# Second mixer's attention: a minimum over negated scores as the exponential's bias, and fillers ahead of each transposition

## The reference

```
# neighbourhood attention, head h
s = q @ k.T * D ** -0.5 + bias[h]            # masked entries: -1e30
p = softmax(s);  o = p @ v
# sliding window attention, head h
s = where(band, q @ k.T * D ** -0.5, -1e30)
m = max(max(s), sink[h])
p = exp(s - m);  denom = sum(p) + exp(sink[h] - m)
o = (p / denom) @ v
# mixer
m = (sigmoid(gate_na) * (o_na @ w_na) + sigmoid(gate_sw) * (o_sw @ w_sw)) @ w_out
```

## Time and profile before

| | us |
|---|---|
| median of three runs | 2382.12 (2380.49 to 2384.36) |
| profiled execution | 2384.57 |
| its span | 2382.70 |
| TensorE busy | 2257.1 (95%) |
| VectorE busy | 1750.5 (73%) |
| ScalarE busy | 1476.7 (62%) |
| GpSimd busy | 236.8 (10%) |

### The profile page before, as it was taken

One profiled execution on the slowest core, in us unless ns is written; L12 is line 12 of the kernel. 1 busy time (PEld: TensorE's weight loads), 2 busy tenths in 40 slices (PEclk: granted clock), 3 DMA queues, 4 the chain that ended last, 5 costly groups with the idle time before them and its releaser, 6 DMA issues.

```text
span 2382.7 us, 31050 instructions
## 1 busy us (share of the span) xinstructions
PE 2257.1 (95%) x11606; PEld 1904.2 (80%) x11606; DVE 1750.5 (73%) x2374; ACT 1476.7 (62%) x2129; POOL 236.8 (10%) x142
## 2 busy tenths in 40 slices
PE   8889999878999999899999889999999999999997
PEld 7677888777788788788789778888888888888885
DVE  6755556773555566655566679999999999999998
ACT  5544445554544455444446568787878887788886
POOL 1431000232000242100215000000000000000000
PEclk9989999999999999999999989999999999999999
DMA  7314555512555534555554379999999999999996
GB/s 283 119 45 156 187 187 175 188 54 81 184 187 187 193 130 151 168 189 187 170 184 142 120 247 359 350 368 347 366 351 369 360 362 356 360 372 366 369 368 245
DMA packets 157276, 570.89 MB, mean 240 GB/s; under 512 B 18561, under 2 KB 18913, under 8 KB 156481
## 3 DMA queue, kind: packets, MB, share of 16 engines
q1 hardware_dynamic: 154032, 555.58, 65.8%
q0 software_dynamic: 3088, 13.27, 1.7%
HBM read 567.72 MB, written 1.05 MB: 239 GB/s over the span
## 4 chain that ended last, share of the span: by engine, by line
PE 84%; DVE 10%; ACT 3%; issue 2%; POOL 0%; DMA 0%; DVEq 0%; SPq 0%; POOLq 0%; ACTq 0%
PE bank L499 23%; PE bank L500 23%; PE bank L501 23%; PE bank L2005 2%; PE bank L2007 2%; PE bank L2006 2%; DVE w_lo L441 2%; PE bank L1631 2%; ACT w_hi L435 1%; PE bank L861 1%; PE bank L1000 1%; PE bank L2562 1%; PE bank L985 1%; DVE X L1889 1%; DVE small L678 1%
## 5 line engine op out<-in xcount | busy, mean ns | idle before, releaser
L441 DVE TENSOR_TENSOR w_lo<-raw,w_hi 128x1024 fp32r<-128x1024 f32 x986 | 1191.3, 1227 | 302.2 <-ACT w_hi L435 272.6
L435 ACT CAST w_hi<-raw 128x1024 fp32r<-128x1024 f32 x1055 | 1100.4, 1051 | 326.0 <-PE bank L501 272.0
L499 PE MATMUL bank<-w_hi,x_hi 128*128 128x512 f32 (+2 forms) x2144 | 843.2, 393 | 27.5 <-DVE w_lo L441 11.4
L500 PE MATMUL bank<-w_lo,x_hi 128*128 128x512 f32 (+2 forms) x2144 | 829.9, 387 | 0.0
L501 PE MATMUL bank<-w_hi,x_lo 128*128 128x512 f32 (+2 forms) x2144 | 829.1, 387 | 0.0
L499 PEld LDWEIGHTS bank<-w_hi,x_hi 128*128 128x128 f32 x2144 | 409.5, 191 | 107.8 <-DVE w_lo L441 9.6
L501 PEld LDWEIGHTS bank<-w_hi,x_lo 128*128 128x128 f32 x2144 | 408.6, 191 | 80.0
L500 PEld LDWEIGHTS bank<-w_lo,x_hi 128*128 128x128 f32 x2144 | 409.7, 191 | 73.7
L441 POOL TENSOR_TENSOR w_lo<-raw,w_hi 128x1024 fp32r<-128x1024 f32 x69 | 165.5, 2408 | 534.6 <-ACT w_hi L435 529.8
L501 PE MATMUL bank<-w_hi,qk_l 128*128 128x512 f32 (+1 forms) x496 | 191.4, 386 | 0.0
L499 PE MATMUL bank<-w_hi,qk_l 128*128 128x512 f32 x448 | 178.1, 398 | 0.2 <-DVE w_lo L441 0.2
(11 more groups left out here) (269 smaller groups left out, 2124.1 us busy)
## 6 DMA issues: line engine op xcount, KB each, us to landing
raw<-in_stream SPq DMA_DIRECT2D x1055, 512.0 KB, 5.7
tab<-in_lngb POOLq DMA_DIRECT2D x5, 1024.0 KB, 8.0
arena<-in_rpb POOLq DMA_DIRECT2D x16, 256.0 KB, 6.8
tab<-in_rowv POOLq DMA_DIRECT2D x2, 640.0 KB, 10.5
X<-in_x SPq DMA_DIRECT2D x1, 1024.0 KB, 5.2
out_y<-X SPq DMA_DIRECT2D x4, 256.0 KB, 2.0
tab<-in_ropec POOLq DMA_DIRECT2D x2, 448.0 KB, 5.4
tab<-in_ropes POOLq DMA_DIRECT2D x2, 448.0 KB, 8.3
```

Source lines behind the costliest of these rows:

```text
L435: nc.scalar.copy(w_hi[:, s % SPLIT, :], raw[:, slot, :]).then_inc(hi_done, 1)
L441: e.tensor_tensor(w_lo[:, s % SPLIT, :], raw[:, s % RAW, :], w_hi[:, s % SPLIT, :].bitcast(F32), ALU.subtract).then_inc(done, 1)
L499: pe.matmul(out, xh, wh, start=first, stop=False)
L500: pe.matmul(out, xh, wl, start=False, stop=False)
```

## The change

It has two parts, both in `paired_attention`.

First, the reduction multiplies the biased scores by -1 and takes the minimum, from the negated sink (`nsinkb`, one small instruction ahead of the loop) or from 3.0e38, and writes it straight to `negm`. The instructions L952 and L953 and the waits between them go. The exponential reads the negated scores with scale -1.

Second, the order within a step: the fillers stand right behind the scaling, then the values of the pair, then the transpositions of head s - 1 and their copy. Before, the transpositions and the copy came first (ScalarE's copy even ahead of the step's exponentials), then the values, then the fillers.

```diff
             for step in range(M + 2):
-                if E.kind == "act" and step % 2 == 1 and step <= M:
-                    copy(step - 1)
...
                         for tb in range(TB):
                             i = e.tensor_tensor_reduce(SS[:, m % 2, tb, :], bank[m % 2][:, tb * S:(tb + 1) * S],
-                                                       a["bias"][:, tb, :], 1.0, -3.0e38, ALU.add, ALU.max,
-                                                       mx[:, 2 * (m % 4) + tb:2 * (m % 4) + tb + 1])
-                        E.link(i)
-                        if "sink" in a:
-                            E.link(e.tensor_scalar(mx[:, sc2], mx[:, sc2], a["sink"], None, ALU.max))
-                        e.tensor_scalar(negm[:, sc2], mx[:, sc2], -a["scale"], None, ALU.mult).then_inc(mx_done, 1)
+                                                       a["bias"][:, tb, :], -1.0, a.get("nsink", 3.0e38),
+                                                       ALU.add, ALU.min,
+                                                       negm[:, 2 * (m % 4) + tb:2 * (m % 4) + tb + 1])
+                        i.then_inc(mx_done, 1)
...
-                                                     bias=negm[:, j:j + 1], scale=a["scale"],
+                                                     bias=negm[:, j:j + 1], scale=-1.0,
...
-                m = step - 1
-                if 0 <= m < M:
-                    if E.kind == "pe":
-                        e.wait_ge(p_scaled, 2 * pairs_before + m + 1)
...
-                        i.then_inc(pt_full, 1)
-                    if E.kind == "dve" and m % 2 == 1:
-                        copy(m)
+                aside(step)
                 if step >= 3 and step % 2 == 1:
                     p = (step - 3) // 2
...
-                aside(step)
+                m = step - 1
+                if 0 <= m < M:
+                    if E.kind == "pe":
+                        e.wait_ge(p_scaled, 2 * pairs_before + m + 1)
...
+                        i.then_inc(pt_full, 1)
+                    if E.kind == ("act" if m % 2 == 0 else "dve"):
+                        copy(m)
...
                 e.wait_ge(bg_in, (l + 1) * 32)
+                E.link(e.tensor_scalar(nsinkb, sinkb, -1.0, None, ALU.mult))
             paired_attention(E, maps, fill, n_pair)
```

More of the change, by code:

```diff
@@ L327, in build @@
         lamv, lame, nlam = sm(2), sm(2), sm(1)
-        sinkb = sm(8)
+        sinkb, nsinkb = sm(8), sm(8)
         sx, negmu, msx, rsx = sm(4), sm(2), sm(2), sm(2)
@@ L1009, in paired_attention @@
                                         ALU.subtract).then_inc(ot_lo, 1)
-                aside(step)
+                m = step - 1
+                if 0 <= m < M:
+                    if E.kind == "pe":
+                        e.wait_ge(p_scaled, 2 * pairs_before + m + 1)
+                        if m:
+                            e.wait_ge(*copied(m - 1))
+                        for kb in range(TB):
+                            for tb in range(TB):
+                                i = e.transpose(bank[2][:, kb * S + tb * P:kb * S + (tb + 1) * P],
+                                                PP[:, m % 2, tb, kb * P:(kb + 1) * P], ident[:, :])
+                        i.then_inc(pt_full, 1)
+                    if E.kind == ("act" if m % 2 == 0 else "dve"):
+                        copy(m)
             E.pa.n += M // 2
@@ L2309, in second_mixer @@
                 j = h // 2
-                maps.append(dict(q=(j, p0, p0 + 64), k=(N_NA + j, p0, p0 + 64), scale=1.0,
+                maps.append(dict(q=(j, p0, p0 + 64), k=(N_NA + j, p0, p0 + 64),
                                  bias=BT[:, h % (NBT - 1)], bias_wait=bias_wait,
@@ L2317, in second_mixer @@
                 maps.append(dict(q=(NH + h // 2, c, c + HD), k=(NH + SH // 2 + kv, c, c + HD),
-                                 scale=1.0, bias=BT[:, NBT - 1], bias_wait=lambda E: None,
-                                 sink=sinkb[:, h:h + 1],
+                                 bias=BT[:, NBT - 1], bias_wait=lambda E: None,
+                                 sink=sinkb[:, h:h + 1], nsink=nsinkb[:, h:h + 1],
                                  v=lambda kb, kv=kv: H2[:, kb, W_H2 - P + kv * HD:W_H2 - P + (kv + 1) * HD],
```

## The result

The changed kernel took 2388.03 us (median of 11 runs, 2380.62 to 2390.68) against 2382.49 (11 runs, 2380.49 to 2384.36): ratio 1.002, 95% interval 1.0012 to 1.0028. It is slower, by 4.8 us (2.9 to 6.7); I had forecast 0.4 us faster. So there is a loss, it is small, and its size is known only to a few us. (A difference in us here is the ratio times the median of before; where medians are subtracted, the text says so.) Of the 22 executions of the changed kernel, these and e10's, 12 ran at a mean granted clock of 0.971 to 0.974 and took 2386.6 to 2390.7 us, and 10 at 0.976 to 0.978 and took 2380.6 to 2386.6; both profiles are of the first kind. The profiled execution took 2388.27 us, its span is 2386.5, 3.8 above that of before.

The account below looks back on a forecast made before the run. TensorE was taken to bound the kernel, its chain covering 84% of the span. Per loop -3.3 + 2.4 + 0.7 = -0.2 us, two -0.4, against the median 2382.12: forecast 2381.7 us, range 2378.0 to 2385.8.

Parts of the forecast that it names:

- front, steps 0 to 13: Loop's front: TensorE waits and slow clock go, 5.0 us, less 1.4 new wait and 0.3 kept: 3.3 us saved a loop.
- order at the end, at full clock: Steps 14 to 17: last transpositions wait 4.4 us for head 14's copy; sliding-window branch starts 2.4 us later a loop.
- half clock behind the last wait: Loop's end: clock expected to fall behind the 4.4 us wait, costing 0.7 us a loop, bounded by nothing and 3.0.
- between the loops: Outside the two attention loops: no instruction changes, so the sum held no term for it.
- The slow one: TensorE's clock falls longer behind the 4.4 and again behind the 1.4: +3.6 us a loop, 2389.3 us; chance 0.07.
- Its point of decision: Both loops: the slower outcome decided by clock losses of 3.3 us a loop on.
- The end is not paid: Loop's end: the 4.4 us wait shrinks or the clock holds; two loops -4.6 us, to 2376.5 us; chance 0.14.
- The one by which GpSimd's hold passes to the scaling: Steps 1 to 4: VectorE and ScalarE chain sets them, half the front's 3.3 lost; 2385.0 us, chance 0.17.

Follow-up runs that it names:

- e10: The changed kernel measured once more, not an instruction altered, against the kernel before: 2384.66 us, ratio 1.0009.
- e6: Changed kernel with 34 extra unused products keeping TensorE busy in the wait ahead of the last transpositions: 2382.14 us, ratio 0.9997 to the kernel before.
- e3: Changed kernel with the first sigmoid and its table load issued in step 16 instead of 15: 2376.11 us, ratio 0.9969 to the kernel before.
- e11: Changed kernel with 14 extra unused products ahead of the sliding-window branch, in the first loop alone: 2385.99 us, ratio 1.0015 to the kernel before.
- e2: Changed kernel with the old reduction (maximum, sink maximum, negation), the new order kept: 2394.00 us, ratio 1.0044 to the kernel before.
- e1: Kernel before with the new reduction alone, the old order of the steps kept: 2379.26 us, ratio 0.9985 to the kernel before.
- e8: Changed kernel with first sigmoid a step later, last values ahead of step 17's halves, third query half and gate biases in step 3: 2376.48 us.

## Why the prediction was wrong

The place and cause of every wait were right, the sizes of the waits too; the clock was not. The terms, for both loops together:

| term | predicted | measured |
|---|---|---|
| front, steps 0 to 13 | -6.6 | -7.3 |
| order at the end, at full clock | +4.8 | +5.2 |
| half clock behind the last wait | +1.4 | +5.0 |
| between the loops | none | +3.0 |
| sum | -0.4 | +5.9 |

- **The front.** Predicted a new wait of 1.4 and no fall of the clock behind it; 1.50 and none. The wait of 0.39 for the rotary embedding, of which I had kept 0.3, is gone, so it gave 3.65 a loop and not 3.3.
- **The end.** Predicted transpositions at +13.2 behind a wait of 4.4, released by L910, then a wait of about 1; measured +13.19, 4.23 and 0.93. The order costs 2.6 by e6, where I had 2.4. e3 shows the cause: with the sigmoid a step later the wait is 1.01. (The wait of 1.45 that I put down to a copy has "issue" in its row. The copy is VectorE's of head 15, which ran from 933.92 to 934.61, right ahead of the values at 934.70.)
- **The step that failed** is the clock's term, "I take 0.7, half of what the first one cost, because the wait itself takes part of it". The half clock began only 0.8 us before the wait of loop 1 ended (929.1, 929.89) and then lasted 6.8 us, twice as long as the one it was scaled from. It cost 2.7 us in loop 1 and 2.25 in loop 2, where it began 1.8 us before the wait's end (1314.8, 1316.62). e6 shows that it is the clock: with the same wait filled it is gone. Nor is the price a fixed one: in loop 2 of e11, the same instructions behind the same wait of 4.23 lose 7.63 - 6.31 = 1.3 us, since the half clock there lasts 3.4. I had its bounds right (nothing to 3.0) and had no reason for a place in them. This error alone, +3.6, would have left the sum at +3.2, inside the range.
- **What was in no term** is the 3.0 us between the loops. I wrote that outside the loops no instruction changes, and took it that no time does. Two spells of half clock there, at 982.6 and 1177.2 before, come later and last 6.8 us instead of 3.4. The first accounts for 2.7 of the 3.0 (from 49 to 208 us behind the loop's end every product is 2.7 later than before), the second for 0.3; e2, where the second alone is long, has 264.27. The first costs so much because it has also left the work that a wait covers. Before, it slows products ahead of transpositions that have to wait for VectorE anyway; in the changed kernel these products run at full clock, the wait is longer, and the half clock begins at 987.1, where nothing covers it. The transpositions in question before, in the changed kernel and in e11:

```profile
988.38 1.32 PE L1906 MATMUL bank<-ident,X 128*128 128x128 f32 x8 [1.23 <-DVE X L1889]
```

```profile
987.87 1.97 PE L1902 MATMUL bank<-ident,X 128*128 128x128 f32 x8 [2.69 <-DVE X L1885]
```

```profile
989.14 1.32 PE L1902 MATMUL bank<-ident,X 128*128 128x128 f32 x8 [1.25 <-DVE X L1885]
```

e11 shows that the moment at which the first loop ends decides it: moved by 1.67 us, both spells last 3.4 again. e1 and e8 have two spells of 3.4 as well, but the first begins 35 us behind the loop's end instead of 30, and the stretch takes 265.5; so the place counts beside the length. Whether every execution has both long spells is open: the ten of the 22 with a mean clock of 0.976 and more suggest that some have not, but none of these was profiled.
- **The rivals.** The slow one had the right sign and, at its end, the right price (3.0 for the clock behind the 4.4); it asked for another fall behind the 1.4, which did not come. The measured loss is short of its +7.2 (4.8 us, or 2.1 in e10). Its point of decision, clock losses of 3.3 a loop, was passed (5.0 + 3.0 over two, 4.0 a loop), but half of that by the stretch between the loops, which it did not name. *The end is not paid* fell with the wait of 4.23. The one by which GpSimd's hold passes to the scaling fell. The groups of the maximum with the sink and of the negation in the first loop before (count, busy time, mean ns of one, idle before):

```profile
L953 DVE TENSOR_SCALAR small<-small 128x2 f32<-128x2 f32 x16 | 10.7, 669 | 0.6
...
L952 DVE TENSOR_SCALAR small<-small 128x2 f32<-128x2 f32 x8 | 7.1, 892 | 0.3
```

and the scaling in the whole changed kernel (shortest/median/longest ns of one):

```profile
L969 DVE TENSOR_SCALAR PP<-PP,small x64: 340/352/546, 836.2 to 1312.3; 128x256 f32<-128x256 f32 x64
```

The hold went with the instructions that had it: 24 of them, of 0.17 to 0.23 us where nothing held them, took 17.8 us, and most of this is VectorE's 16. It lay under TensorE's work. The scaling stayed at 0.35 us, 0.55 at most, so the hold did not pass to it.

On the clock, the traces show a fall behind 4.23 each time, none behind 1.50 alone, one behind 1.32, 0.30 and 1.31 before and none behind e1's 0.91, 1.67 and 0.17, a fall in one loop of two behind e2's 2.10 and 2.05, in one of four behind 1.00 and 0.83, and 16 times of 24 behind the untouched 2.28. The Trainium skill, page TensorE: Matmul & The Clock Gate, section Part 1: The HAM clock gate, says that the chip watches TensorE in windows that run on by themselves and do not start with the kernel; e8's two loops and e11 agree. The same page's advice, to avoid long idle gaps, would not have been enough here: e8's clock fell behind 1.00 and 0.83.

## What to carry to other kernels

When an order moves a copy that TensorE waits for behind long work on its own engine (here a table load and a sigmoid, 3.2 us), move that work and not the copy: one step later was worth 9 to 12 us here, by the medians. Price a new TensorE wait by bounds, from no half clock behind it to the longest spell on record (6.8 us here, 2.7 us of time), and not by one scaled from a shorter spell elsewhere: the same wait of 4.23 cost 1.3, 2.25 and 2.7 us. And a forecast of under 0.2% in a kernel whose clock falls now and then needs a wider range, since shifting a stage's end by 1.7 us moved a stretch of 264 us that holds no changed instruction by 3.

## What the runs showed of the hardware

- The length of a half-clock spell in the same work was 3.4 or 6.8 us, by when the stage before it ended (e11 against the changed kernel). What the longer and later spells cost was 2.7 us at the first place between the loops and 0.3 at the second, so a spell has no price of its own: it depends on the waits that it falls on.
- One and the same wait of TensorE, 2.28 us behind each loop, was met by half clock 16 times of 24.
- At half clock the branch's products followed each other at 0.21 us instead of 0.12 (930.99 to 931.20 and 936.04 to 936.16 in the changed kernel), so a spell costs less than half of its length. As an estimate from these steps, (0.21 - 0.12) / 0.21, a us of half clock costs 0.43 where TensorE has no waits: 2.6, 2.2 and 1.2 us for the 6.0, 5.0 and 2.9 us of it behind the last wait (loops 1 and 2 of the changed kernel, loop 2 of e11), where 2.7, 2.25 and 1.3 were measured.
- Thirty-four unused products in a wait of 4.2 us, which shortened nothing, made the kernel 2.5 to 5.9 us faster by the medians (e6 against the two measurements of the changed kernel). The 2.5 are of the same session, and the intervals touch there (up to 1.0007, from 1.0000); the profile is the firmer ground, both loops 2.0 to 2.5 us shorter and the stretch between them 2.9.
- The reduction costs 0.41 us from start to start with the negated sink as its start value (917.71 to 918.12) and 0.34 with a constant (866.00 to 866.34). This was the unknown that I had bounded by 0.2.
